# Filling TensorE's waits around four norms with matmuls whose result nobody reads

## What is computed

```python
for i in range(2):
    mod = (silu(c) @ ada_w[i] + ada_b[i])[:, None, :]
    sh1, sc1, g1, sh2, sc2, g2 = jnp.split(mod, 6, axis=-1)
    h = rmsnorm_2(x, norm_mix[i]) * (1 + sc1) + sh1
    x = x + g1 * mixer_i(h)                       # projection, attention, projection out
    h = rmsnorm_2(x, norm_ffn[i]) * (1 + sc2) + sh2
    x = x + g2 * swiglu_2(h, ffn_w_in[i], ffn_w_out[i])
```

## Time and profile before

| what | us |
|---|---|
| runs: median (lowest to highest) | 1900.13 (1899.7 to 1907.81) |
| profiled execution, its own time | 1892.05 |
| its span, first to last instruction | 1890.3 |
| TensorE busy in it | 1747.8 (92%) |
| mean granted TensorE clock | 0.967 |

### The profile page before, as it was taken

One profiled execution on the slowest core, in us unless ns is written; L12 is line 12 of the kernel. 1 busy time (PEld: TensorE's weight loads), 2 busy tenths in 40 slices (PEclk: granted clock), 3 DMA queues, 4 the chain that ended last, 5 costly groups with the idle time before them and its releaser, 6 DMA issues.

```text
span 1890.3 us, 31178 instructions
## 1 busy us (share of the span) xinstructions
PE 1747.8 (92%) x12350; PEld 1571.3 (83%) x12350; DVE 1280.5 (68%) x2298; ACT 837.8 (44%) x1663; POOL 84.1 (4%) x154
## 2 busy tenths in 40 slices
PE   4899988899999999998788999988899998989998
PEld 3699867898888888898677999786899887879996
DVE  1426778558887666667775888868678785675554
ACT  3523664242222222444653544356544435665442
POOL 1000124000000000001030000000000000000000
PEclk8899999899999999999788999999999999999999
DMA  9363111056556655333333998743399874416653
GB/s 323 110 202 89 29 46 46 23 152 180 173 169 199 186 176 169 123 114 96 118 107 105 264 275 262 248 133 69 112 281 273 271 245 132 125 45 179 183 176 132
DMA packets 355232, 299.59 MB, mean 158 GB/s; under 512 B 8256, under 2 KB 325424, under 8 KB 354960
## 3 DMA queue, kind: packets, MB, share of 16 engines
q1 hardware_dynamic: 353664, 293.44, 50.9%
q0 software_dynamic: 1424, 4.16, 0.9%
HBM read 296.52 MB, written 1.05 MB: 157 GB/s over the span
## 4 chain that ended last, share of the span: by engine, by line
PE 79%; DVE 9%; ACT 4%; DMA 4%; issue 4%; SPq 0%; DVEq 0%; ACTq 0%
PE bank L1035 77%; PE bank L1049 2%; ACT whigh L1706 1%; DMA AWH<-in_w_ada 1%; DVE wlow L2293 1%; DMA raw<-in_w_down 1%; DVE A L2746 1%; ACT A L1982 1%; DVE ACC L2309 1%; DMA raw<-in_ffn_w_out 0%; DMA raw<-in_ffn_w_in 0%; DVE nmax L2719 0%; DMA raw<-in_w_up 0%; DVE PTA L2753 0%; DMA AWH<-in_ada_w 0%
## 5 line engine op out<-in xcount | busy, mean ns | idle before, releaser
L2293 DVE TENSOR_TENSOR wlow<-raw,whigh 128x2048 fp32r<-128x2048 f32 (+2 forms) x183 | 409.9, 2244 | 258.9 <-ACT whigh L1706 258.4
L1706 ACT ACTIVATE whigh<-raw 128x2048 fp32r<-128x2048 f32 (+2 forms) x183 | 343.0, 1877 | 291.7 <-PE bank L1035 96.8
L1035 PE MATMUL bank<-HTH,whigh 128*128 128x256 f32 (+1 forms) x1440 | 445.6, 309 | 5.4 <-issue 5.4
L1035 PE MATMUL bank<-HTH,wlow 128*128 128x256 f32 (+1 forms) x1440 | 442.0, 307 | 0.0
L1035 PE MATMUL bank<-HTL,whigh 128*128 128x256 f32 (+1 forms) x1440 | 441.9, 307 | 0.0
L1035 PE MATMUL bank<-whigh,HTH 128*128 128x256 f32 (+1 forms) x1008 | 294.9, 293 | 21.6 <-DVE HTL L2616 6.3
L1035 PE MATMUL bank<-wlow,HTH 128*128 128x256 f32 (+1 forms) x1008 | 290.4, 288 | 0.0
L1035 PE MATMUL bank<-whigh,HTL 128*128 128x256 f32 (+1 forms) x1008 | 290.2, 288 | 0.0
L1035 PEld LDWEIGHTS bank<-HTH,whigh 128*128 128x128 f32 x1440 | 275.1, 191 | 17.9 <-issue 5.9
L1035 PEld LDWEIGHTS bank<-HTH,wlow 128*128 128x128 f32 x1440 | 275.0, 191 | 12.5
L1035 PEld LDWEIGHTS bank<-HTL,whigh 128*128 128x128 f32 x1440 | 275.2, 191 | 11.8
(11 more groups left out here) (247 smaller groups left out, 2210.8 us busy)
## 6 DMA issues: line engine op xcount, KB each, us to landing
raw<-in_ffn_w_in SPq DMA_DIRECT2D x88, 512.0 KB, 5.4
A<-in_ada_w SPq DMA_DIRECT2D x38, 1024.0 KB, 6.9
A<-in_w_ada SPq DMA_DIRECT2D x28, 1024.0 KB, 5.5
raw<-in_w_gate SPq DMA_DIRECT2D x44, 512.0 KB, 5.4
raw<-in_w_up SPq DMA_DIRECT2D x44, 512.0 KB, 6.4
raw<-in_ffn_w_out SPq DMA_DIRECT2D x20, 1024.0 KB, 5.1
raw<-in_w_in SPq DMA_DIRECT2D x18, 1024.0 KB, 6.9
raw<-in_w_down SPq DMA_DIRECT2D x18, 1024.0 KB, 5.6
```

What stands on the lines that cost most here:

```text
L1035: return nc.tensor.matmul(out, lhsT, rhs, start=start, stop=stop, skip_group_check=True)
L1706: nc.scalar.activation(parts(loads[n])[0], raw_slot(loads[n]), ACT.Copy).then_inc(*made("split_high", loads[n]))
L2293: V.tensor_tensor(low, raw_slot(loads[n]), as_float(high), ALU.subtract).then_inc(*made("split_low", loads[n]))
```

## The change

`fill(b, n)` issues n matmuls of EYE (stationary) with the first 512 columns of DISTR (moving) into a bank, each of which starts afresh; nothing reads the result. It is called in three places of each of the four norms: in `norm_turn` ahead of the second half's transposes (`FILL_TURN`: 6, 5, 8, 5), in `norm_spread` between the gate row and the wait for the roots (`FILL_ROOT`: 6), and at the first products (`FILL_FIRST`: 7).

```diff
+FILL_TURN = {(1, "ffn"): 6, (2, "ffn"): 5, (3, "mix"): 8, (3, "ffn"): 5}
+FILL_ROOT = 6
+FILL_FIRST = 7
...
+            def fill(b, n):
+
+                pe.wait_ge(*upto("dist_in"))
+                for _ in range(n):
+                    mm(bank[b], EYE[:, :], DISTR[:, 0, :], True, True)
...
             def norm_turn(l, st, g, h):
 
                 at = [open_bank("h", l, st, g, 2 * h + b) for b in range(2)]
+                if h == 1:
+                    fill(count.banks["h", l, st, g, 2], FILL_TURN[l, st])
                 for t in range(2):
...
             def norm_spread(l, st):
 
                 gate_row(l, st, 0, 0)
+                if NBANKS in holder:
+                    pe.wait_ge(*drained(*holder[NBANKS]))
+                fill(NBANKS, FILL_ROOT)
                 pe.wait_ge(*upto("rooted", l, st, 0))
                 ps = open_bank("r", l, st)
...
                     if l == 3 and (at, n) == (0, 0):
                         for t2 in X_TILES:
                             ahead[t2] = open_bank("u", l, j, t2)
+                        fill(count.banks["u", l, j, 0], FILL_FIRST)
                         for k in range(KD):
                             need_h(l, "mix", 0, k)
...
                         for g, name in enumerate(("gate", "up")):
                             if (u, k) == (0, 0):
                                 opened[f, name] = open_bank(name, l, f)
+                                if l and name == "up":
+                                    fill(count.banks["up", l, f], FILL_FIRST)
                             last = mm3(opened[f, name][:, r], (wh[:, g, k, :], wl[:, g, k, :]), (HTH[:, k, r], HTL[:, k, r]),
                                        k == 0, k == KD - 1)
```

## The result

| | before | after |
|---|---|---|
| median of 20 runs (lowest to highest), us | 1905.73 (1899.22 to 1915.65) | 1912.97 (1904.6 to 1918.4) |
| ratio, 95% interval | | 1.0036 (1.0024 to 1.0048) |
| profiled execution / span, us | 1892.05 / 1890.3 | 1906.47 / 1904.7 |

The change costs 0.36%, some 6.9 us (interval 4.6 to 9.1). With more runs the median of before is 5.6 us above the one that stood ahead of the prediction. The two profiled executions lie 14.4 us apart, and what exceeds the 6.9 us has to be sorted out first. Here are TensorE's busy time after, which answers to the earlier trace rows, and the two long unbroken stretches of the chain that ended last, which answer to the earlier trace rows.

What follows compares the result with a forecast made beforehand. The prediction took TensorE's own order as the bound. Its terms, 0.8 us ahead of the transposes, 2.9 ahead of the roots and 4.8 at the first products, sum to 8.5 us: 1908.6 us, +0.45%, range 1901.5 to 1914.5.

Steps and rivals of the forecast that it cites:

- The bound: TensorE, busy 92% of the span; coming late out of a norm, it stays late through long unbroken stretches behind.
- The price of a matmul: Each added 128x512 fp32r matmul costs 0.227 us, as in a long run of them; upper bound 0.315 us.
- The 0.315 of the pairs: Price in us of the table matmuls multiplied today two at a time between other shapes, kept as upper bound.
- Ahead of the transposes: Blocks before the second half's transposes make them 0, 0.3, 0.5 and 0 us late in the four norms, 0.8 in all.
- one for one: A late second group of transposes delays the gate row behind it, and so the next block, by the same time.
- Ahead of the roots: The block takes 1.36 us against room of 0.62 to 0.66; spreading the roots starts late, 2.9 us over four norms.
- At the first products: In three feed-forward parts the block stands behind the wait, 1.59 us each, 4.8 in all; in (3, mix) it fits, 0.
- The sum: 0.8 + 2.9 + 4.8 = 8.5 us over the four norms; upper bound 14.2 us.
- The clock: TensorE's granted clock reads 1.00 over all four norms of the profiled execution, so there nothing is to be won.
- clock rival: Falls of the clock in the four norms of timed executions are prevented, 6.4 us back, leaving +2.1 us; chance 0.14.
- The sentence of the Trainium skill: By this rule the norms would look almost idle, the clock would fall in each, and the sum would be +2.1 us.
- dear matmuls: Rival: the added matmuls cost 0.315 us each, +14.2 us, 1914.3 us, slower; chance 0.12.

Runs made afterwards that it cites:

- first_triple: Changed kernel with FILL_FIRST 21 in place of 7 and no matmuls at the other two places; ratio 1.0084 (1.0061 to 1.0107) against the kernel before.
- turn_only: Changed kernel with only the blocks ahead of the transposes (6, 5, 8, 5), other sizes 0; ratio 1.0000 (0.9980 to 1.0019) against the kernel before.
- changed_again: The changed kernel without any edit, run again; ratio 1.0041 (1.0022 to 1.0060) against the kernel before.
- fit: Changed kernel with blocks cut or moved to the room in the waits, FILL_ROOT 2, turn sizes 6, 3, 4, 4; ratio 0.9994 (0.9977 to 1.0010) against before.
- fit_b: The same kernel as fit, run again; ratio 1.0011 (0.9995 to 1.0026) against the kernel before.
- first_only: Changed kernel with only the 7 at the first products, other sizes 0; ratio 1.0024 (1.0007 to 1.0041) against the kernel before.

## Why the prediction was right

- **The bound.** TensorE comes late out of a norm and stays late: the stretches of the chain behind the norms (1, ffn) and (3, ffn) grew by exactly the block in them, and the 17.1 us forecast for first_triple came out as 16 in the timed runs (12 to 20).
- **The price of a matmul.** 0.227 us taken, 0.229 measured at the first products. Ahead of the roots it is 0.232: the gate row starts at 1041.38 and its eight take 0.112 us each, so the six have 1042.27 to 1043.67, the start of the products with rs, 1.39 us from unrounded starts. The 0.315 of the pairs is no price of a longer block; why a pair is that dear was not tried.
- **Ahead of the transposes.** 0, 0.3, 0.5, 0 forecast; 0, 0.28, 0.50, 0 measured. Its rule "one for one" holds only while the block ahead of the roots is there; turn_only shows the room swallowing it.
- **Ahead of the roots.** 2.9 us forecast. The lateness of the products was 3.0, of which 2.6 reach the first product. This term was 0.3 us too big: it passed the whole lateness on, while 0.1 us a norm comes back in the products with rs.
- **At the first products.** 3 x 1.59 = 4.8 us forecast, 3 x 1.60 measured, 4.84 us won back by moving the block. (3, mix): the block fits in the wait, as forecast.
- **The sum.** 8.5 us forecast, 8.06 in the traces of the changed kernel, 6.9 (4.6 to 9.1) in the timed runs.
- **The clock.** Here the prediction was too sure. It read 1.00 over four norms of one execution and said there was nothing to win. Its clock rival (a fall in every norm, 6.4 us back) is wrong in size, but falls in the norms of before do exist: four in 20 norms, on average 5.1 / 5 = 1.0 us per execution. One of the prediction's own signs of being wrong has thus come about, a norm of before under 1.00 while after is at 1.00; its step "nothing is to be won" rested on one execution. If the blocks prevent all such falls, 8.06 - 1.0 = 7.0 us are left; if none, 8.06. Timed are 6.9 (4.6 to 9.1) and 7.8 us (4.2 to 11.4), which fit both. That the blocks prevent falls is not shown. Were falls as frequent with blocks in all three places as elsewhere, the eight seen in 56 norms would all miss those 20 in about 2 of 100 draws, but would miss the 14 with every wait filled in about 8 of 100, and the groups were formed after the falls had been seen.
- **The sentence of the Trainium skill** (TensorE: Matmul & The Clock Gate, Part 4: PE-mode transpose) that transposes don't count as busy in the same way: taken as a rule that every such norm sees a fall, it is not borne out, with 16 of 20 norms of before at 1.00. The prediction also called transposes half the work in these norms. Between the last product ahead of norm (1, ffn) and the first behind it they are 8 of 28 matmuls, so the norms would not look almost idle without them. Whether transposes count for less was not tried.
- **The level.** The base of 1900.13, from three runs, was low: 1905.73 over 20 runs. The forecast time, 1908.6, is therefore 4.4 us under the 1912.97 measured, although the cost was put too high. That 1912.97 still lies in the range of 1901.5 to 1914.5 owes something to luck: its upper end was set for dear matmuls, which did not come. Also the span forecast for the profile after, 1899, was 1904.7, by the 3.5 and 2.8 us outside the norms. The profiled execution of before was a fast one. In the 35 runs of before that the first experiments timed the mean granted clock is 0.962, against 0.967 in it, and a straight line through these runs gives 1.3 us for each 0.001. That makes some 6.5 of the 13.7 us between it and the median of 20 runs; the rest is open. Mean clocks with blocks (0.961 in changed_again, 0.962 in fit and fit_b) are not higher than without (0.961 to 0.962), so whatever falls the blocks may spare are a small part of all.

## What to carry to other kernels

Work put in to fill a wait must stand ahead of the waiting instruction in the engine's order and be no longer than the room: on an engine that is the bound, what is over the room or behind the wait is paid nearly in full, unless a later wait still has room. Size it by the starts in the trace, counting that a group's modelled end is later than the moment at which the next can start. Before buying insurance against a rare event, look at several executions: one trace with no fall in four norms did not mean that there are none, and the worth, if every fall were prevented, was still only 1.0 us against a premium of 8.

## What the runs showed that was not expected

A wait on a semaphore that was met long before is not free when it stands directly ahead of the wait that ends last. With blocks of size 0, `fill` leaves its wait on "dist_in" (and, where bank 6 has a last reader, a second one) ahead of the wait for the roots. In first_only the products with rs then started 0.20 us later than before in (1, ffn) and (3, mix), which have two such waits, and 0.09 in (2, ffn) and (3, ffn), which have one. In turn_only, which has the same waits, it is again 0.20 and 0.09, counted from the root's end. VectorE's last step of the root, and the first product with rs, in norm (1, ffn) of first_only:

```profile
1042.37 0.16 DVE L2360 SCALAR_TENSOR_TENSOR rs<-nw,rs 128x2 f32<-128x2 f32 x1
```

```profile
1042.79 0.68 PE L1038 MATMUL bank<-ident,rs 128*128 128x128 f32 x4 [0.65 <-ACT A L1827]
```

From the root's end, 1042.53, to the product are some 0.25 us, where before it was 0.06. In fit, with two matmuls between those waits and the last one, it is 0.06 again. What causes it stays open.
